# Two-block transformer kernel: paired weighing, later half panels and sooner head norms in the last attention, and the gate's spatial products set between the panels

## The reference, cut to what matters

```python
# second block, layer 0: the gate (gMLP mixer); S = 512 tokens = 4 chunks of 128, D = 1024
uv = gelu(h @ w_in);  u, v = split(uv)
v = layer_norm_gain(v, v_gain)                         # over the 1024 columns of a token
z = einsum('gts,bcsgd->bctgd', w_sp * causal, v)       # 8 groups g of 128 columns, 128x128 weights
z = z + b_sp
out = (u * z) @ w_out
# second block, layer 1: differential attention, 8 heads, 2 halves i of 64 columns
s = einsum('bhitd,bhisd->bhits', q, k) * scale + bias  # bias = -slope[h] * distance, causal
p = softmax(s)
a = p[:, :, 0] - lam * p[:, :, 1]
o = einsum('bhts,bhsd->bhtd', a, v)                    # v has 128 columns per head
o = rms_norm_2(o, subln) * (1 - lambda_init)           # over the 128 columns of a head
x = x + o.reshape(B, S, V_WIDTH) @ w_o
```

## Time and profile before

| | us |
|---|---|
| median of three runs | 1921.3 |
| lowest and highest run | 1918.41, 1923.67 |
| profiled execution | 1920.69 |
| span of its records | 1918.9 |
| PE busy | 1884.2 (98% of the span) |
| DVE, ACT, POOL busy | 1086.7, 769.4, 260.2 |

### The profile page before, as it was taken

One profiled execution on the slowest core, in us unless ns is written; L12 is line 12 of the kernel. 1 busy time (PEld: TensorE's weight loads), 2 busy tenths in 40 slices (PEclk: granted clock), 3 DMA queues, 4 the chain that ended last, 5 costly groups with the idle time before them and its releaser, 6 DMA issues.

```text
span 1918.9 us, 25130 instructions
## 1 busy us (share of the span) xinstructions
PE 1884.2 (98%) x8884; PEld 1545.5 (81%) x8884; DVE 1086.7 (57%) x1567; ACT 769.4 (40%) x1181; POOL 260.2 (14%) x206
## 2 busy tenths in 40 slices
PE   7999999999999999999999999999999999999998
PEld 6877778788878888888888888888787888888886
DVE  5867876677767525566544442254867564444223
ACT  4226655355555314543323332144555433332212
POOL 4703320020000002101100000022643010000001
PEclk9999999999999999999999999999997999999998
DMA  4232232122222322221222222222111122222222
GB/s 178 89 109 78 96 103 66 55 99 97 89 98 92 121 94 99 88 88 66 99 98 87 98 98 99 98 98 99 56 56 34 55 99 92 101 92 98 99 98 77
DMA packets 62838, 174.48 MB, mean 91 GB/s; under 512 B 5429, under 2 KB 23989, under 8 KB 62649
## 3 DMA queue, kind: packets, MB, share of 16 engines
q1 hardware_dynamic: 61424, 169.50, 25.6%
q10 hardware_dynamic: 1016, 2.92, 0.5%
q0 software_dynamic: 336, 1.25, 0.2%
HBM read 171.54 MB, written 2.10 MB: 90 GB/s over the span
## 4 chain that ended last, share of the span: by engine, by line
PE 91%; DVE 4%; ACT 2%; issue 1%; POOL 1%; DMA 1%; SPq 0%; POOLq 0%; DVEq 0%; ACTq 0%
PE ps L457 29%; PE ps L458 29%; PE ps L459 29%; PE ps L973 1%; DVE w_lo L1630 1%; POOL square_sum L2392 1%; DMA w_raw<-in_weights 1%; PE ps L984 1%; ACT w_hi L1079 1%; DVE at_e L1858 0%; PE ps L928 0%; PE ps L477 0%; PE ps L661 0%; PE ps L652 0%; DVE result L2375 0%
## 5 line engine op out<-in xcount | busy, mean ns | idle before, releaser
L1630 DVE TENSOR_TENSOR w_lo<-w_raw,w_hi 128x1024 fp32r<-128x1024 f32 x315 | 402.0, 1276 | 477.8 <-ACT w_hi L1079 477.2
L457 PE MATMUL ps<-xg_hi,w_hi 128*128 128x512 f32 (+1 forms) x1448 | 565.1, 390 | 11.3 <-DVE w_lo L1630 10.0
L458 PE MATMUL ps<-xg_lo,w_hi 128*128 128x512 f32 (+1 forms) x1448 | 558.4, 386 | 0.0
L459 PE MATMUL ps<-xg_hi,w_lo 128*128 128x512 f32 (+1 forms) x1448 | 558.1, 385 | 0.0
L1079 ACT ACTIVATE w_hi<-w_raw 128x1024 fp32r<-128x1024 f32 x315 | 331.6, 1053 | 536.5 <-PE ps L459 530.7
L457 PEld LDWEIGHTS ps<-xg_hi,w_hi 128*128 128x128 f32 x1448 | 272.8, 188 | 77.2 <-DVE w_lo L1630 17.1
L459 PEld LDWEIGHTS ps<-xg_hi,w_lo 128*128 128x128 f32 x1448 | 272.6, 188 | 54.6
L458 PEld LDWEIGHTS ps<-xg_lo,w_hi 128*128 128x128 f32 x1448 | 272.9, 188 | 53.6 <-issue 1.0
L457 PE MATMUL ps<-hid_hi,w_hi 128*128 (+1 forms) x528 | 205.7, 390 | 0.0
L459 PE MATMUL ps<-hid_hi,w_lo 128*128 (+1 forms) x528 | 205.5, 389 | 0.0
L458 PE MATMUL ps<-hid_lo,w_hi 128*128 (+1 forms) x528 | 205.5, 389 | 0.0
(11 more groups left out here) (353 smaller groups left out, 2524.1 us busy)
## 6 DMA issues: line engine op xcount, KB each, us to landing
w_raw<-in_weights SPq DMA_DIRECT2D x315, 512.0 KB, 3.2
out_cols<-result SPq DMA_DIRECT2D x8, 256.0 KB, 2.2
x<-in_x_cols SPq DMA_DIRECT2D x2, 512.0 KB, 5.1
x<-in_x_cols SPq DMA_DIRECT2D x1, 1024.0 KB, 8.2
squares<-in_mem_cols ACTq DMA_DIRECT2D x1, 512.0 KB, 3.8
sp_w<-in_spatial ACTq DMA_DIRECT2D x1, 512.0 KB, 4.3
sp_b<-in_spatial_bias ACTq DMA_DIRECT2D x1, 512.0 KB, 5.2
dil<-in_dil_table POOLq DMA_DIRECT2D x1, 448.0 KB, 9.3
```

Of the source, the lines that this page charges most:

```text
L457: nc.tensor.matmul(to, wh, xh, start=start, stop=False)
L458: nc.tensor.matmul(to, wh, xl, start=False, stop=False)
L459: return nc.tensor.matmul(to, wl, xh, start=False, stop=stop)
L1630: nc.vector.tensor_tensor(w_lo[:, u % 2, :], w_raw[:, u % 2, :], w_hi[:, u % 2, :].bitcast(F32), ALU.subtract).then_inc(w_ready, 1)
```

## The change

Five parts.

1. **Gate.** Two spatial groups stand behind each of the panels 4, 5, 6 and 7, instead of all eight after panel 7, in four banks (4 to 7). DVE's z, product and lo of these groups stand between the panels too. ACT's square root for v's norm and the split of unit u0+3 stand ahead of the first Gelu; the spatial weights are split before the second half of v.
2. **Weighing in pairs.** `weigh(n-6)` is done at odd n only, for two query blocks at once: for the first j the right side is 256 columns (both blocks), for the last j 128 (only the later block attends to it). Per head that is 18 matmuls instead of 30, 12 of them 256 columns wide. The turned weights of a pair lie side by side, those of the first pair in a new buffer `da_late` (or, for the last head, in `xg_hi`, `xg_lo`, chunk 7).
3. **Half panels.** Each stands one item later: item 0 has none, item 26 has one. A panel's output and split move from even to odd items.
4. **Head norm of heads 0 to 3.** The squares of head 3 stand at item 22, `heads_turned` at the end of PE's item 24, spreads 0 and 1 at the end of item 25, spreads 2 and 3 at the end of item 26, in banks 2 and 3. The output columns stand in items 29, 30, 32 and 34.
5. **Bias.** POOL multiplies the bias between staging k and staging q.

In the code after, the lines of the same steps are L472 to L474 (product), L998 (scores), L1009 (turn), L1666 (`w_lo`), L2305 (least), L2321 (probs), L2330 (`lo`), L2380 (`head_normed`), L2385 (`head_lo`), L972 and L973 (spread).

```diff
-        return n % 2 == 0 and 0 < n <= 2 * (2 * N_DIFF - EARLY_PANELS)
+        return n % 2 == 1 and 1 < n <= 2 * (2 * N_DIFF - EARLY_PANELS) + 1
...
-        BO_EARLY = 4 * N_DIFF - 2
+        BO_EARLY = 4 * N_DIFF - 3
         COLUMN_ITEMS = (BO_EARLY, BO_EARLY + 1, BO_EARLY + 3, BO_EARLY + 5)
...  PE, gate
-            for g in range(N_SPATIAL):
-                if g >= 2:
-                    pe.wait_ge(a_in["z"], g - 1)
+            def spatial_group(g):
+                if g == 0:
+                    pe.wait_ge(a_in["w_lo"], 1)
+                if g >= 4:
+                    pe.wait_ge(a_in["z"], g - 3)
...
+            for p in range(2, KC):
+                pe.wait_ge(a_in["scaled"], p - 1)
+                panel(u0 + p, None, ps[:, 2 + p % 2, :], xg_hi, xg_lo)
+                if p == SPATIAL_FROM:
+                    pe.wait_ge(a_in["v"], 2 * TB)
+                if p >= SPATIAL_FROM:
+                    spatial_group(2 * (p - SPATIAL_FROM))
+                    spatial_group(2 * (p - SPATIAL_FROM) + 1)
...  PE, an item of the last attention
             def head_sums(h):
                 pe.wait_ge(a3["sq"], h + 1)
+                if h == 4:
+                    pe.wait_ge(a3["normed"], 3)
...
                 def weigh(n):
-                    s, b = n // TB, n % TB
+                    s, pair = n // TB, n % TB // 2
                     pe.wait_ge(a3["pt"], n + 1)
...
-                    for j in range(b + 1):
+                    hi, lo = turned_pair(s, pair)
+                    last = 2 * pair + 1
+                    for j in range(last + 1):
                         cols = slice(j * P, (j + 1) * P)
-                        mm = product(ps[:, 6, b * P:(b + 1) * P], vh[:, cols], vl[:, cols],
-                                     at3["pt_hi"][:, n % 2, cols], at3["pt_lo"][:, n % 2, cols], j == 0, j == b)
+                        one = j == last
+                        mm = product(ps[:, 6, (2 * pair + one) * P:2 * (pair + 1) * P].rearrange("p (b n) -> p b n", n=P), vh[:, cols], vl[:, cols],
+                                     hi[:, j, one:, :], lo[:, j, one:, :], j == 0, j == last)
                     mm.then_inc(a3["pv"], 1)
...
+                p = EARLY_PANELS + (n - 1) // 2
+                if n and p < 2 * N_DIFF:
+                    if n % 2 and n > 1:
+                        pe.wait_ge(kv["qk"], p)
+                    half_panel(qk0 + p, ps[:, 7, :], *qk_input(p), (n - 1) % 2)
+                if n in COLUMN_ITEMS:
+                    output_column(COLUMN_ITEMS.index(n))
+                if live(n - 6) and n % 2:
+                    weigh(n - 6)
+                if n == 23:
+                    head_sums(3)
+                if n == 24:
+                    heads_turned(0, 3)
                 if n == 25:
-                    heads_turned(0, 3)
+                    head_spread(0, 2)
+                    head_spread(1, 3)
                 if n == 26:
-                    pe.wait_ge(kv["qk"], 2 * N_DIFF)
-                    head_spread(0, 7)
-                if n == 27:
-                    head_spread(1, 3)
                     pe.wait_ge(a3["normed"], 1)
-                    head_spread(2, 7)
-                if n == 28:
+                    head_spread(2, 2)
                     pe.wait_ge(a3["normed"], 2)
                     head_spread(3, 3)
-                p = EARLY_PANELS + n // 2
-                if p < 2 * N_DIFF:
-                    if n % 2 == 0 and n:
-                        pe.wait_ge(kv["qk"], p)
-                    half_panel(qk0 + p, ps[:, 7, :], *qk_input(p), n % 2)
...  DVE, an item of the last attention
                 if n == 26:
-                    head_normed(0, 7)
+                    head_normed(0, 2)
+                    head_normed(1, 3)
                 if n == 27:
-                    head_normed(1, 3)
-                    head_normed(2, 7)
+                    head_normed(2, 2)
+                    head_normed(3, 3)
                     head_lo(0)
+                    head_lo(1)
                 if n == 28:
-                    head_normed(3, 3)
-                    head_lo(1)
                     head_lo(2)
-                if n == 29:
                     head_lo(3)
...  POOL
                 for k, name in enumerate(("k", "q")):
+                    if k:
+                        if not first_pair:
+                            pool.wait_ge(a3["least"], at(8 * (s - 1), c, 16))
+                        nc.gpsimd.tensor_tensor(da["bias"][:, s, :], da["alibi"][:], column("slopes", at(s, c, 2)).to_broadcast([P, BAND]),
+                                                ALU.mult).then_inc(a3["bias"], 1)
                     pool.wait_ge(kv["qk"], at(2 * s + k + 1, c, 4))
```

224 lines of the change are left out of this document (121 added, 103 removed).

## The result

The changed kernel takes **1906.7 us** in the median of four runs (1905.88 to 1907.94), the kernel before 1921.5 in the same comparison. The ratio is 0.9925, with an interval of 0.9908 to 0.9942: 14.7 us faster. The profiled execution took 1905.88 us, with a span of 1904.0.

The account below looks back on a forecast made before the run. PE bounds the kernel, busy for 98% of the span. Gate -9.0, pairs -3.9, tail -3.3, start +1.0 and bias 0 sum to -15.2 us: 1906.0 against the median of 1921.3, range 1899 to 1914.

Parts of the forecast that it names:

- Gate, -9.0: Gate: spatial matmuls at full clock -6.7, first residual matmuls -1.3, no wait for `w_lo` about -1.0; sum -9.0 us.
- slack near zero behind panel 7: Gate: DVE's w_lo for the residual's third unit done 13.5 us after panel 7, just when PE needs it; counted 0.
- Pairs up to item 22, -3.9: Last attention up to item 22: weighing in pairs saves 1.05 us per head, less waits at even items; -3.9 us.
- rival C: Weighing: a matmul twice as wide costs twice the time, so pairing brings nothing; 1914 us, chance 0.05.
- +0.5 for waits at even items: Last attention: no weighing covers DVE's panel output at even items, so PE waits at up to ten panels; +0.5 us.
- Start, +1.0: Item 0 of the last attention: PE idles 3 us, which may lower the clock behind it; +1.0 us, bounds 0 and +2.5.
- one of my own signs: Last attention: the clock falling in its panels, where before it never did, would make the prediction wrong altogether.
- Tail, -3.3: Item 23's turn to output column 4: -6.3 at full clock, +3 for a clock fall lasting 6 us; -3.3 us.
- my own case (60.4): Tail: the distance from item 23's turn to output column 4 is 60.4 us, 3.3 less than before.
- rival A: Tail: the clock stays down as long as before, so the tail gains 0; 1909.3 us, chance 0.20.
- Bias, 0: POOL's bias (1.68 us) ahead of q's copies, while POOL waits for q's panel anyway; no step on PE, 0 us.
- Rival D: Last attention: next head's q staged too late; up to 1929 us, chance 0.03 slower, 0.05 for losing 3 to 8 us.

Follow-up runs that it names:

- Experiment 2: The changed kernel with each pair weighed as two blocks of 128 columns, 30 matmuls per head instead of 18: 1915.4 us.
- Experiment 3: The changed kernel with twelve matmuls of 512 columns, whose result nobody reads, added in item 0 where PE waits: 1904.4 us.
- experiment 10: The kernel before with the gate's part, the weighing in pairs and POOL's bias between k's and q's staging, nothing else: 1896.0 us.
- experiment 9: The changed kernel with the head norm and output columns of the first heads at the items of before: 1898.7 us.
- experiment 7: The kernel before with the gate's part and the weighing in pairs, nothing else: 1898.6 us.

## Why the prediction was right, and which of its terms were not

The forecast was 1906.0, the measured time 1906.7, well inside the range. The sum held because one term was right and the errors of the others cancelled: against the forecast, pairs up to item 22 brought 1.8 us more, the start cost 1.8 more and the tail brought 1.4 less, and 0.6 ahead of the gate's u panels and 0.8 behind column 4 stand in no term at all. That the total came within 1 us is luck.

**Gate, -9.0: right in size and mechanism.** The timelines stand 9.3 apart at the first scores, of which 8.7 are the gate's; the gate alone measures -10.0. The terms: the parcels take 2.62 each, so 6.7 less, as worked out; the residual's start gained 1.2 (forecast 1.3); the eight panels take 0.8 less, since the wait of 0.82 for `w_lo` is gone (forecast 1.0). The slack near zero behind panel 7 showed no wait.

**Pairs up to item 22, -3.9: too small.** The failed step is the price of a head before, 3.15 us. It took the short first step of 0.06 off each parcel of weighing, while rival C in the same prediction counts 30 x 0.112 = 3.36. Experiment 2 decides for 3.36: at full clock, its items 0 to 22 need 5.1 us more than the changed kernel's, 1.27 for each of the four heads, and 3.36 - 2.1 is 1.25. And the +0.5 for waits at even items did not come: no such wait is in the trace. With both put right the term is -5.3. (Its own figures, -4.2, -0.3 and +0.5, give -4.0 and not -3.9.) Between the scores of item 1 and item 23's turn the changed kernel takes 98.5 us with a clock of 0.97, so 95.6 at full clock against 101.3 before: -5.7. Experiment 3, which has full clock there, confirms it with 95.7 (1330.15 to 1425.84). Of this the width is the larger part (experiment 2). The last 0.4 stay open.

**Start, +1.0: too small.** The wait came as forecast (2.92 of 3.0) and the next scores stand as far behind the first as before. The mis-sized term is the clock: 2.8 us (experiment 3), above my upper bound of 2.5. The reason I gave for a value near the lower end, that half panels follow, is wrong: they followed, and ran at 0.50. By that one of my own signs came true, a clock that falls in the panels of the last attention, by which the prediction would be wrong altogether; the fall cost no more than these 2.8. Nor is the price a fixed one: in experiment 2, with the same wait of 2.92 us, the clock fell only at 1332.7 and for 3.4 us instead of 6.8.

**Tail, -3.3: it was -1.9.** The work at full clock was forecast at 49.4 and is about 49.2 (61.8 - 6.95 - 5.6). The new idle was forecast at 8, at the right places (items 25, 28 and 29, and the sums of head 4), and measured 6.95. The clock was forecast to cost 3 and cost about 5.6. The step that failed is "a fall that lasts 6 us": the fall that began at 1455.4, between the wait at item 28's turn and that for the sums of head 4, lasted 10.2 us, and a second one of 3.4 came at 1475.9, behind a wait of 0.94 at item 32's turn. The stretch took 61.8 us, between my own case (60.4) and rival A (63.7), somewhat nearer to my own.

**Bias, 0: not shown to be 0.** I called it covered, and looked only at whether q would be late. Rival D did not appear: no wait on POOL's staging in the trace. What I missed is the other direction. The bias no longer runs beside the four-block probs on DVE, and in the order of before that is worth 2.6 us (experiment 10). The earlier trace rows had shown it: a probs of 2.00 us from 1458.97 on, and POOL's row beside it, before, was this:

```profile
1458.74 1.67 POOL L2503 TENSOR_TENSOR da_bias<-alibi,par 128x896 f32<-128x896 f32 x1
```

The four-block probs of the last attention up to the tail's first half, before (window 1340 to 1475) and then after (1340 to 1465):

```profile
L2276 DVE SCALAR_TENSOR_TENSOR at_e<-at_e,at_inv 128x512 f32<-128x512 f32 x6 | 11.6, 1935 | 0.0
```

```profile
L2321 DVE SCALAR_TENSOR_TENSOR at_e<-at_e,at_inv 128x512 f32<-128x512 f32 x6 | 4.5, 747 | 0.0
```

The parts of the change together took them from 1.94 to 0.75 us in the mean. Part of it moved: those of three blocks went from 0.61 to 0.79 and those of one block from 0.55 to 0.79. In the changed kernel itself the bias was not undone, so how much of it lies in the 1906.7 stays open.

**What the prediction never asked** is whether each part is worth having. I priced the tail as one sum of old work and new waits. The sooner norm alone costs 8 us (experiment 9), 7.2 of them there, hidden in a sum that came out negative only since pairing takes 8.5 away in that stretch (experiment 7). Experiment 9 against 10 adds that the later half panels, with the norm back in its place, cost 2.7; in the traces 2.8 of it lie in items 0 to 22, as much as item 0's lost clock. Without both, the same edits give 1896.0.

## What to carry to other kernels

A part that moves work must be priced against the kernel with the other parts and without it, not against the kernel before: a gain elsewhere hides what it costs. Where PE's stretches are thin, what stands on DVE between two results that PE needs is PE's time, and each us of waiting can cost another through the clock, so count both. And in a stream of matmuls with new weights for each, width was nearly free here: 256 columns took 0.12 us and 128 took 0.11. Why the narrow ones are no faster, no run here shows.

## What the runs showed of the hardware that I had not expected

- A single wait of 2.9 us brought the clock from 1.00 to 0.50 for the half panel of 512-column matmuls behind it, though what came before was full work up to the first scores; with the wait filled by matmuls that nobody reads the clock was 1.00. The wait's price was so doubled, 2.9 idle and 2.8 slow. In experiment 2 the same wait was followed by a shorter fall, 3.4 us instead of 6.8. In the gate, with parcels of 128-column matmuls between its panels and no wait, the clock stayed at 1.00 for 28 us.
- A probs with both inputs in SBUF took 0.75, 1.27 and 1.91 us in the same place of three kernels, by what POOL did beside it. The Trainium skill, "SBUF — State Buffer", section Who interferes with whom, says that a DVE instruction with two SBUF inputs contends with a GpSimd instruction that reads SBUF. The trace agrees: 1.91 lies beside POOL's 1.68 us bias (experiment 7), 0.75 beside nothing (experiment 9).
